# A chain of layers on one core: three units read tile by tile at the end of a stage, low halves written over the loaded weights, four high halves

## What is computed

```python
# first block
for layer in range(2):
    mix = gla_mixer(h, ...) if layer == 0 else diff_attention(h, ..., k1, k2, v, ...)
    h = layer_norm(ALPHA * h + mix, ...)
    ffn = hier_moe(h, ...)            # 4 groups of 4 experts, 512 hidden units each
    h = layer_norm(ALPHA * h + ffn, ...)
# second block
for l in range(2):
    x = layer_norm_2(ALPHA * x + 0.5 * swiglu(x, ffn1_gate[l], ffn1_up[l], ffn1_down[l]), ...)
    mix = ...                          # short convolution, gated MLP, sparse attention, then @ w_out[l]
    x = layer_norm_2(ALPHA * x + mix, ...)
    x = layer_norm_2(ALPHA * x + 0.5 * swiglu(x, ffn2_gate[l], ffn2_up[l], ffn2_down[l]), ...)
```

## Time and profile before

| | |
|---|---|
| median of 3 runs | 1987.91 us (1985.16 to 1994.66) |
| the profiled execution | 1987.95 us |
| its span, first to last instruction | 1986.1 us |
| PE busy | 1904.5 us (96%) |
| DVE, ACT, POOL busy | 1280.7, 1010.5, 138.5 us |
| granted PE clock, mean | 0.978 |
| read from HBM | 422.95 MB, 213 GB/s |

### The profile page before, as it was taken

One profiled execution on the slowest core, in us unless ns is written; L12 is line 12 of the kernel. 1 busy time (PEld: TensorE's weight loads), 2 busy tenths in 40 slices (PEclk: granted clock), 3 DMA queues, 4 the chain that ended last, 5 costly groups with the idle time before them and its releaser, 6 DMA issues.

```text
span 1986.1 us, 22115 instructions
## 1 busy us (share of the span) xinstructions
PE 1904.5 (96%) x9262; PEld 1577.2 (79%) x9262; DVE 1280.7 (64%) x1283; ACT 1010.5 (51%) x1081; POOL 138.5 (7%) x114
## 2 busy tenths in 40 slices
PE   7989999997999999997999999999999999999998
PEld 5768888886988888886888787788878887877886
DVE  3456888887676988988544547655454545675544
ACT  4544776774563766764443346444334433644442
POOL 1012000002003000001000210200010003011000
PEclk8998999998999999999999989999999999999999
DMA  8434998997434988996655462465565555335551
GB/s 293 149 106 169 345 343 320 347 335 245 166 129 143 364 317 321 362 325 250 225 182 177 152 204 85 151 210 190 171 209 186 168 196 187 107 128 192 190 175 58
DMA packets 221009, 425.59 MB, mean 214 GB/s; under 512 B 8648, under 2 KB 29392, under 8 KB 220896
## 3 DMA queue, kind: packets, MB, share of 16 engines
q1 hardware_dynamic: 214992, 405.87, 58.6%
q0 software_dynamic: 5904, 18.17, 3.0%
HBM read 422.95 MB, written 1.06 MB: 213 GB/s over the span
## 4 chain that ended last, share of the span: by engine, by line
PE 90%; DVE 5%; ACT 2%; issue 1%; POOL 1%; DMA 0%; POOLq 0%; SPq 0%; DVEq 0%; ACTq 0%
PE ps L431 25%; PE ps L433 25%; PE ps L432 25%; DVE Wlo L402 2%; PE ps L539 1%; PE ps L1394 1%; PE ps L1418 1%; ACT Whi L390 1%; PE ps L2233 1%; PE ps L2327 1%; PE ps L2297 1%; DVE X L639 1%; POOL rs L633 1%; PE ps L1218 1%; PE ps L1451 1%
## 5 line engine op out<-in xcount | busy, mean ns | idle before, releaser
L402 DVE TENSOR_TENSOR Wlo<-raw,Whi 128x2048 fp32r<-128x2048 f32 (+1 forms) x382 | 863.0, 2261 | 527.6 <-ACT Whi L390 527.4
L390 ACT ACTIVATE Whi<-raw 128x2048 fp32r<-128x2048 f32 (+1 forms) x391 | 736.4, 1886 | 501.2 <-PE ps L433 491.6
L431 PE MATMUL ps<-Whi,XTh 128*128 128x512 f32 (+2 forms) x1760 | 684.3, 389 | 29.5 <-DVE XTl L551 27.2
L433 PE MATMUL ps<-Whi,XTl 128*128 128x512 f32 (+2 forms) x1760 | 670.9, 381 | 0.0
L432 PE MATMUL ps<-Wlo,XTh 128*128 128x512 f32 (+2 forms) x1760 | 670.8, 381 | 0.0
L431 PEld LDWEIGHTS ps<-Whi,XTh 128*128 128x128 f32 x1760 | 337.0, 191 | 97.8 <-issue 17.8
L433 PEld LDWEIGHTS ps<-Whi,XTl 128*128 128x128 f32 x1760 | 336.4, 191 | 63.0
L432 PEld LDWEIGHTS ps<-Wlo,XTh 128*128 128x128 f32 x1760 | 337.3, 192 | 60.8 <-issue 1.7
L431 PE MATMUL ps<-Whi,hTh 128*128 128x512 f32 x608 | 239.2, 393 | 0.0
L433 PE MATMUL ps<-Whi,hTl 128*128 128x512 f32 x608 | 236.9, 390 | 0.0
L432 PE MATMUL ps<-Wlo,hTh 128*128 128x512 f32 x608 | 236.7, 389 | 0.0
(11 more groups left out here) (307 smaller groups left out, 1456.0 us busy)
## 6 DMA issues: line engine op xcount, KB each, us to landing
raw<-in_moe_w_gate SPq DMA_DIRECT2D x64, 1024.0 KB, 6.1
raw<-in_moe_w_up SPq DMA_DIRECT2D x64, 1024.0 KB, 6.2
raw<-in_moe_w_down SPq DMA_DIRECT2D x64, 1024.0 KB, 6.7
raw<-in_ffn_gate SPq DMA_DIRECT2D x44, 1024.0 KB, 5.0
raw<-in_ffn_up SPq DMA_DIRECT2D x44, 1024.0 KB, 5.0
raw<-in_ffn_down SPq DMA_DIRECT2D x40, 1024.0 KB, 4.9
raw<-in_w_in SPq DMA_DIRECT2D x18, 1024.0 KB, 5.0
raw<-in_a_w_in SPq DMA_DIRECT2D x12, 1024.0 KB, 10.9
```

What stands on the lines that cost most here:

```text
L390: act.activation(Whi[:, i % NS, 0:m * n], raw[:, i % NR, 0:m * n], ACT.Copy).then_inc(w_rounded, tick(w_rounded, "rounded", i))
L402: dve.tensor_tensor(Wlo[:, i % NS, 0:m * n], raw[:, i % NR, 0:m * n], h.bitcast(f32), ALU.subtract).then_inc(w_rest, tick(w_rest, "rest", i))
L431: pe.matmul(o, xh(k, t), h[:, q, :], start=k == first, stop=False)
L433: x = pe.matmul(o, xl(k, t), h[:, q, :], start=False, stop=k == end)
```

## The change

- **Memory.** NR is 7 and NS is 4. Wlo has no memory of its own: the low half of unit i is written over the loaded unit, in `raw[i % NR]`. So SP may load unit i only when PE has used unit i-7.
- **Stage ends.** `hold` is now a number of units. At the end of stages 1, 5, 6, 7, 8, 9 and 10 the last three units are taken together, all for tile 0 and then all for tile 1, and (not at stage 10) PE's transposes of tile 0 stand ahead of the last unit of tile 1. Stages 2, 3 and 4 keep two units, with the transposes at the end.
- **Order on DVE.** In `sum_done_dve` the low half of XT for tile 0 now stands ahead of the sums of tile 1.
- **Tile 1's turn.** In the next stage PE's transposes of tile 1 stand three quarters into the second unit of tile 0 (into the only unit, after stage 2), no longer behind it. After stages 1 and 3 they stay where they were.
- **Look-ahead.** Whatever was rounded up to unit z + NS is now one unit further. The first stage rounds units 1 and 2 early, as before.

```diff
-    NR, NS = 5, 3
+    NR, NS = 7, 4
-    Wlo = at_("Wlo", [128, NS, 2048], f32r, lo_o)
+    Wlo = at_("Wlo", [128, NR, 2048], f32r, raw_o)
...
             if i >= NR:
-                sp.wait_ge(*on("rest", i - NR))
+                sp.wait_ge(*on("used", i - NR))
...
+    def job_pe(pe, name, xh, xl, ready, nt=2, skew=False, hold=0, second=None, turn=None):
         bs = [bank(pe, name, t, hold=True) for t in range(nt)]
         nk = units[jobs[name][0]][4]
+        last = jobs[name][-1]
         for z, group in enumerate(groups(name, skew, hold)):
             for t in range(nt):
                 for i in group:
-                    use_unit(pe, i, t, bs[t], xh, xl, ready, 0, nk - 1)
-                if t == 0:
-                    yield z - 0.5
+                    if turn and t == nt - 1 and i == last:
+                        turn()
+                    here = second and z == 0 and t == 0 and i == group[-1]
+                    use_unit(pe, i, t, bs[t], xh, xl, ready, 0, nk - 1, 3 * units[i][1] // 4 if here else None, second)
...
+    def sum_done_act(act, v):
+        round_units(act, last_unit(v) + 2)
+        x_turn_act(act, v, 0)
 
     def sum_done_dve(dve, v, t, split=True):
-        if t == 0:
-            norm_a_dve(dve, v, 0)
-            norm_b_dve(dve, v, 0)
-            return
-        if split:
+        if t == 1:
+            stats_dve(dve, 1, 1)
+        norm_a_dve(dve, v, t)
+        norm_b_dve(dve, v, t)
+        if t == 0 and split:
             rest_units(dve, last_unit(v) + 2)
             x_turn_dve(dve, v, 0)
-        stats_dve(dve, 1, 1)
-        norm_a_dve(dve, v, 1)
...
+    def outer_pe(pe, v, name, ready, order=(0, 4), hold=3):
         js = jobs[name]
         bs = [[bank(pe, name, t, hf, hold=True) for t in range(2)] for hf in range(2)]
+
+        def use(i, t):
+            use_unit(pe, js[i], t, bs[i % 2][t], xt_h, xt_l, ready, order[0], order[1] + 3)
+        for i in range(4 - hold):
+            for t in range(2):
+                use(i, t)
+            yield i
+        for t in range(2):
+            for i in range(4 - hold, 4):
+                if (t, i) == (1, 3) and hold == 3:
+                    x_turn_pe(pe, v, 0)
+                use(i, t)
         for hf in range(2):
-            for t in range(2):
-                use_unit(pe, js[hf], t, bs[hf][t], xt_h, xt_l, ready, order[0], order[1] + 3)
-            yield hf
-        for t in range(2):
-            for hf in range(2):
-                use_unit(pe, js[2 + hf], t, bs[hf][t], xt_h, xt_l, ready, order[0], order[1] + 3)
-                held.discard(bs[hf][t])
-            sum_done_pe(pe, v, t)
+            held.difference_update(bs[hf])
+        if hold == 2:
+            x_turn_pe(pe, v, 0)
...
-        for z in job_pe(pe, ("fdown", a, l, 1), ht_h, ht_l, h_ready, hold=True):
+        turn_0 = (lambda: x_turn_pe(pe, v, 0)) if split else None
+        for z in job_pe(pe, ("fdown", a, l, 1), ht_h, ht_l, h_ready, hold=3, turn=turn_0):
             pass
-        sum_done_pe(pe, v, 1, split)
...
-        for z in outer_pe(pe, 3, ("df", "out"), o_ready):
+        for z in outer_pe(pe, 3, ("df", "out"), o_ready, hold=2):
```

More of the change, by code:

```diff
@@ L368, in groups @@
             if hold:
-                gs_[-2:] = [gs_[-2] + gs_[-1]]
+                gs_[-hold:] = [sum(gs_[-hold:], [])]
             elif skew:
@@ L417, in load_units, with use_unit @@
             if i >= NR:
-                sp.wait_ge(*on("rest", i - NR))
+                sp.wait_ge(*on("used", i - NR))
             sp.dma_start(raw[:, i % NR, 0:m * n].rearrange("p (t n) -> p t n", n=n), ap).then_inc(
                 w_landed[i % NR], tick(w_landed[i % NR], "landed", i, by=16))
-    def use_unit(pe, i, t, b, xh, xl, ready, first, end):
+    def use_unit(pe, i, t, b, xh, xl, ready, first, end, at=None, what=None):
         _, m, n, k0, _ = units[i]
@@ L428, in use_unit @@
         for q in range(m):
+            if q == at:
+                what()
             k = k0 + q
@@ L740, in ffn_pe @@
         for c in range(6):
-            for z in job_pe(pe, ("fgate", a, l, c), xt_h, xt_l, ready, skew=c == 0):
-                if c == 0 and z == -0.5:
-                    second_pe(pe, v - 1)
+            second = (lambda: second_pe(pe, v - 1)) if c == 0 else None
+            for z in job_pe(pe, ("fgate", a, l, c), xt_h, xt_l, ready, skew=c == 0, second=second):
                 if c > 0 and z == 0:
@@ L779, in ffn_act @@
                 turn(5)
[L780 removed]
+        for z in job_act(act, ("fdown", a, l, 1), None, hold=3):
             pass
[L782 removed]
+        if split:
+            sum_done_act(act, v)
     def ffn_dve(dve, a, l, v, split=True):
@@ L1516, in moe_pe @@
             for hf in range(2):
-                for z in job_pe(pe, ("down", l, g, hf), hh, hl, h_ready, 1, hold=g == 3 and hf == 1):
+                for z in job_pe(pe, ("down", l, g, hf), hh, hl, h_ready, 1, hold=2 if (g, hf) == (3, 1) else 0):
                     if z == 0 and hf == 0:
@@ L1559, in evac @@
                     free(act_done, name, t)
-                for z in job_act(act, name, evac, 1, hold=g == 3 and hf == 1):
+                for z in job_act(act, name, evac, 1, hold=2 if (g, hf) == (3, 1) else 0):
                     if z == 0 and hf == 0:
@@ L1594, in moe_dve @@
             for hf in range(2):
-                for z in job_dve(dve, ("down", l, g, hf), None, 1, hold=g == 3 and hf == 1):
+                for z in job_dve(dve, ("down", l, g, hf), None, 1, hold=2 if (g, hf) == (3, 1) else 0):
                     if z == 0 and hf == 0:
@@ L1855, in o_ready @@
                 pe.wait_ge(*on("lo", "doT", k // 4, t))
-        for z in job_pe(pe, ("df", 0, 0), xt_h, xt_l, ready, skew=True):
-            if z == -0.5:
-                second_pe(pe, 2)
+        for z in job_pe(pe, ("df", 0, 0), xt_h, xt_l, ready, second=lambda: second_pe(pe, 2)):
+            pass
         job_w_pe(pe, ("df", 1, 0), ready)
@@ L1999, in diff_act @@
         router_act(act, 1)
-        for z in outer_act(act, 3, ("df", "out")):
+        for z in outer_act(act, 3, ("df", "out"), hold=2):
             if z == 0:
@@ L2133, in diff_dve @@
         router_dve(dve, 1)
-        for z in outer_dve(dve, 3, ("df", "out")):
+        for z in outer_dve(dve, 3, ("df", "out"), hold=2):
             if z == 0:
@@ L2376, in run @@
             return job_pe(pe, ("mx", l, n), xt_h, xt_l, ready, **k)
-        for z in run("kv", skew=True):
-            if z == -0.5:
-                second_pe(pe, v - 1)
+        for z in run("kv", skew=True, second=lambda: second_pe(pe, v - 1)):
+            pass
         for z in run("q"):
```

59 lines of the change are left out of this document (20 added, 39 removed).

## The result

The changed kernel takes 1968.07 us (median of 5 runs, 1967.07 to 1972.09) against 1990.56 us of the kernel before (5 runs by then, 1985.16 to 1994.66): a ratio of 0.9891, 95% interval 0.9869 to 0.9914. That is 1.1% faster, and the interval stays clear of 1; the prediction counted 0.5% as the least that can be told from no change. The forecast was 1974.8 us with a range of 1966.5 to 1984.0. Between the two profiled executions the difference is 20.9 us (1987.95 to 1967.07), where the sum had 13.2. The measured time is within the range, but only 1.6 us above its lower end.

A forecast was written before the change was run, and what follows sets the result against it. PE, busy 1904.5 us, was taken to bound the kernel, so only its idle and low-clock time could move. Gains of 21.0 us less losses of 7.8 made 13.2 off 1987.95: 1974.8 us, range 1966.5 to 1984.

The forecast's parts named there:

- Ends of 5 to 9: PE's idle time around both tiles' turns shrinks: 2.7 us gained at each of 5, 7, 8; 1.8 at 6 and 9.
- First stage: ACT's low rank copy now stands behind a later unit's load, so PE's L864 moves to about 36.9: 2.7 us lost.
- End of 3: POOL's unit goes ahead of DVE's X (3.8 us), plus 0.8 for a bank and 0.5 for resting: 5.1 us lost.
- the first rival: Losses keep more: clock low longer at stages 1 and 3, first stage loses 4; 1981.5 us, chance 0.2.
- End of 1: The idle 1.92 us at stage 1's end goes; its second turn already had cover: 2.1 us gained.
- The clock term: Behind stage 1's end, the 149.39 to 159.63 stretch at clock 0.50: half of the possible 5.1, 2.5 us gained.
- Copies: In stages 6 and 9 PE's wait for a DVE copy behind two subtractions goes: 0.95 us each, 1.9 gained.
- End of 2: A subtraction leaves the path, but POOL's early unit delays DVE's X: 0.3 us, plus 0.7 at second turn, 1.0 gained.
- Loads: Loads now wait for PE's use of unit i-7; in expert stages 12 us against 6.1 to landing: costed at nothing.
- The slow rival: POOL's unit meets tile 0's X at every end, X 4.2 us later at six ends: 2000 us, chance 0.07.
- the ends of 4 to 9: Gains at the stage ends: 1.8 us at 4, 2.7 each at 5, 7 and 8, 1.8 each at 6 and 9.

The follow-up runs named there:

- one wait: The changed kernel with POOL starting its unit only when DVE has finished X of tile 0: 1955.85 us, ratio 0.9844.
- Two runs with the same instructions from 40 us on: The changed kernel with POOL's unit behind X of tile 0 (1955.85 us), and that plus a first-projection look-ahead of three units, not four (1954.87 us).

## Why the prediction was right, and where its sizes were off

- **Ends of 5 to 9.** Right: 2.8 and 1.9 us for 2.7 and 1.8. What remains is 0.15 and 0.28 us, not 0.4 and 0.4. The order needs the fourth high half for it: alone it gives 0.4 to 0.5.
- **First stage.** Right, L868 at 36.84 for a forecast of 36.8, and undoing it alone gives 2.8 us, of which 2.3 are seen in that stage.
- **End of 3.** The mechanism was right to the row: 5.48 us beside POOL, 3.70 idle before the turn, 2.01 for the bank. The term that was mis-sized is the sentence that left the stretch at 0.50 as long as it was. It doubled, and another of 3.4 us stands behind it, so 5.1 became 7.8. I had this in the first rival ("up to 3 us more at 0.50") and not in the sum.
- **End of 1.** Its 2.1 us is right. The clock term took half of the possible 5.1 because nothing told which; the step of 6.9 leaves 4.8 for it. The stretch went whole. That it went so was in part luck: three other kernels with this end keep 3.4 us of it.
- **Copies.** 0.95 us each was right; the half of 3.4 us at 0.50 behind each, and some 0.3 more, was not thought of. Together with the last two points, the step that fell short is one: idle time was costed as idle time, and the slow matmuls behind it were costed only where a long stretch already stood in the rows.
- **End of 2.** The step that failed is "POOL's unit is now rounded before the root is done". I had carried it over from stage 4. ACT was idle for 6.26 us there, by "issue", before it rounded. Rows of before had a hint, the rounding at 473.48 behind the same kind of idle time (3.38 us), and I had not looked at it. What ACT waits for behind its branch stays open.
- **Loads.** Costed at nothing, and right for seven units; but the reason, 6 us of cover, was wrong. A margin in the time of one load says little where the DMA engines are busy for 0.94 of the time: five units, which by that reasoning should have cost up to 1 us on some loads, cost 122 us.
- **The slow rival.** POOL did not meet X at every end. The 1.0 us that I had counted in DVE's favour was 1.2, and it is the order that makes it: with the same buffers in the old order POOL meets X at every end but that of stage 2, and the time is 2024 us.

The sum was thus right for the ends of 4 to 9 and the first stage. It came out 7.7 us short, because most of the errors were of one sign: clock 2.3 at stage 1 and 4.1 at the copies, 2.4 at stage 2, 0.8 in small pieces, 0.8 behind the end of stage 9, less 2.7 at stage 3.

## What to carry to other kernels

A buffer more can make a kernel slower: it lets a side engine start earlier, and if that work shuts out an instruction on the critical path, as POOL's unit and DVE's X do here, POOL ahead by 0.13 us made X 4.2 us longer, at eight of nine stage ends. So say in the program who goes first; one wait was worth 12 us here, more than half of the whole change. And when you cost a stop of PE, cost what follows it as well: many stops of 1 to 5 us came with 3 to 14 us of matmuls at half clock. Last, ask of a buffer count how busy the queue is, not only how long one load takes.

## What the runs showed of the hardware that I had not expected

- A small change in a stop could change the stretch at a granted clock of 0.50 behind it by much: stage 1's went from 10.24 us to none, stage 3's from 6.83 to 13.65 and 3.41 and, with the wait, back to 6.83.
- Two runs with the same instructions from 40 us on had different stretches at two places, worth some 3 us each. The runs of these two kernels spread over 5.3 and 6.9 us, so this is of the size of that spread, and it bounds what one profile can settle.
- The gain of a removed stop can come from what stands behind it: the copy in stage 6 waited for 0.95 us, and its passage gave 3.0. The two parts also came singly there: 1.4 us with the wait gone and the stretch as long as before, 1.6 with the wait still there and the stretch 3.4 us shorter.
- DVE's X and POOL's unit shut each other out in both orders: 5.4 to 5.5 us in place of 1.28 for X behind POOL, 5.17 in place of 4.55 for POOL 0.48 us behind X.
